# Seven half-tile products in the second and third part of the first two feed forwards, their modulation moved into the first part, and a gate activation scaled by GpSimd

## What is computed

```
def swiglu(h, w_gu, w_down):
    g, u = jnp.split(h @ w_gu, 2, axis=-1)
    return (jax.nn.silu(g) * u) @ w_down
...
        h = h + swiglu(rms_norm(h, f_norm[layer]), f_w_gu[layer], f_w_down[layer])
```

## Time and profile before

| | us |
|---|---|
| median of 3 runs | 2104.94 (2104.70 to 2105.11) |
| the profiled execution | 2104.22 |
| its span, first to last instruction | 2102.3 |
| TensorE busy | 2074.3 (99%) |
| TensorE weight loads busy | 1675.8 (80%) |
| VectorE busy | 1137.5 (54%) |
| ScalarE busy | 813.9 (39%) |
| GpSimd busy | 863.0 (41%) |

### The profile page before, as it was taken

The page is one execution under the profiler, slowest core; times in us unless marked ns, Lnnn a source line. Parts: engine busy times, 40 slices in busy tenths (PEclk is TensorE's granted clock), DMA queues, the critical chain, the costliest instruction groups (busy, mean ns, idle before and its releaser), DMA issues.

```text
span 2102.3 us, 27305 instructions
## 1 busy us (share of the span) xinstructions
PE 2074.3 (99%) x10570; PEld 1675.8 (80%) x10570; DVE 1137.5 (54%) x1785; ACT 813.9 (39%) x1243; POOL 863.0 (41%) x644
## 2 busy tenths in 40 slices
PE   8999999999999999999999999999999999999999
PEld 6888888888888444888888878676778888989898
DVE  6445542343354797445325355576664847749393
ACT  4123221222323787322122245564454535435252
POOL 5545655555542211455556534322223240342333
PEclk9999999999999999999999999999999999999999
DMA  4224333432541000243343231211112122233232
GB/s 174 100 100 150 120 140 138 160 114 77 192 131 55 21 1 7 105 159 135 130 155 120 84 123 60 81 41 60 58 43 80 42 83 98 71 111 111 91 108 93
DMA packets 35529, 206.20 MB, mean 98 GB/s; under 512 B 4192, under 2 KB 5344, under 8 KB 16096
## 3 DMA queue, kind: packets, MB, share of 16 engines
q1 hardware_dynamic: 33408, 197.89, 26.2%
q10 hardware_dynamic: 2016, 6.88, 1.0%
HBM read 200.63 MB, written 2.10 MB: 96 GB/s over the span
## 4 chain that ended last, share of the span: by engine, by line
issue 39%; PE 32%; POOL 27%; ACT 1%; DVE 0%; DMA 0%; POOLq 0%; SPq 0%; DVEq 0%; ACTq 0%
POOL WL L523 27%; PE PS L1274 9%; PE PS L895 2%; PE PS L926 2%; PE PS L908 2%; PE PS L1340 2%; PE PS L1341 2%; PE PS L1342 2%; PE PS L634 2%; PE PS L636 2%; PE PS L635 2%; PE PS L718 1%; PE PS L720 1%; PE PS L719 1%; PE PS L825 1%
## 5 line engine op out<-in xcount | busy, mean ns | idle before, releaser
L523 POOL TENSOR_TENSOR WL<-WR,WH 128x512 fp32r<-128x512 f32 (+2 forms) x528 | 703.9, 1363 | 887.2 <-ACT WH L1409 887.2
L634 PE MATMUL PS<-Hh,WH 128*128 128x512 f32 x1152 | 451.8, 392 | 9.2 <-DVE Hl L2052 7.9
L1409 ACT ACTIVATE WH<-WR 128x2048 fp32r<-128x2048 f32 (+2 forms) x133 | 237.6, 1786 | 561.5 <-PE PS L636 521.1
L635 PE MATMUL PS<-Hl,WH 128*128 128x512 f32 x1152 | 449.4, 390 | 0.0
L636 PE MATMUL PS<-Hh,WL 128*128 128x512 f32 x1152 | 449.3, 390 | 0.0
L634 PEld LDWEIGHTS PS<-Hh,WH 128*128 128x128 f32 x1152 | 216.9, 188 | 56.3 <-issue 9.0
L635 PEld LDWEIGHTS PS<-Hl,WH 128*128 128x128 f32 x1152 | 217.0, 188 | 45.8 <-issue 1.0
L636 PEld LDWEIGHTS PS<-Hh,WL 128*128 128x128 f32 x1152 | 217.0, 188 | 45.5
L634 PE MATMUL PS<-Gh,WH 128*128 128x512 f32 x416 | 161.8, 389 | 0.0
L635 PE MATMUL PS<-Gl,WH 128*128 128x512 f32 x416 | 161.8, 389 | 0.0
L636 PE MATMUL PS<-Gh,WL 128*128 128x512 f32 x416 | 161.8, 389 | 0.0
(11 more groups left out here) (354 smaller groups left out, 3717.7 us busy)
## 6 DMA issues: line engine op xcount, KB each, us to landing
WR<-wA SPq DMA_DIRECT2D x125, 1024.0 KB, 4.8
AW<-wada SPq DMA_DIRECT2D x24, 1024.0 KB, 6.9
...
```

The costliest lines, as they stand in the source:

```text
L523: ins = nc.gpsimd.tensor_tensor(WL[:, s, piece], WR[:, s, piece], WH[:, s, piece].bitcast(F32), ALU.subtract)
L634: nc.tensor.matmul(PS[:, b, :], wh[:, c, cols], pe_h, start=c == 0, stop=False)
L635: nc.tensor.matmul(PS[:, b, :], wh[:, c, cols], pe_l, start=False, stop=False)
L1409: nc.scalar.activation(WH[:, s, 0:n], WR[:, s, 0:n], ACT.Copy).then_inc(hi_s, 1)
```

## The change

- The feed forwards of layers 0 and 1 are made in three parts, of 8, 8 and 6 hidden tiles, as that of layer 2 is. The first part stays plain; all of the second and third part (14 units of each layer) are made of seven products.
- In these units `gate_sums` gets a second instruction, the multiplication with the row of inverse roots (now `RSF`), which waits for the first. The multiplication after the silu is given to GpSimd (`scale_gate`), and `gated` waits for it.
- GpSimd's order in a part: from the third unit on, the scaling for unit n-2 comes ahead of the two weight sums of unit n; the scalings of the last two units come after the last sums, ahead of the low parts of the down weights.
- All 12 modulation units of a layer are done in its first part: one behind each of the 8 gate and up units, four among the first part's down products. The two sums of one share an output buffer, so the second waits for the first. SyncE issues their loads accordingly.
- In the first part GpSimd also adds high and low input together (`whole_inputs`, eight 128x512 additions behind the third and fourth unit), VectorE makes the four sums of token halves (behind the fourth unit) and their low parts (behind the sixth and seventh), ScalarE the high parts.
- The down weights of the first part use other buffers (`DNH`, `DNL` for odd units). The weights of the second part's first unit can be put in place after seven of the eight down tiles.
- In layer 2 the instructions stay; the host lays the weights out in quarters for the new units.

```
 SEGMENTS = [
     ("win", "A", 12), ("wout", "A", 4),
-    ("gu0a", "A", F1), ("dn0a", "B", 8), ("gu0b", "A", F2), ("dn0b", "C", 8),
+    ("gu0a", "A", 8), ("dn0a", "D", 8), ("gu0b", "A", 8), ("dn0b", "D", 8), ("gu0c", "A", 6), ("dn0c", "E", 8),
     ("wq", "A", 4), ("wkv", "A", 6), ("wo", "A", 4),
-    ("gu1a", "A", F1), ("dn1a", "B", 8), ("gu1b", "A", F2), ("dn1b", "C", 8),
+    ("gu1a", "A", 8), ("dn1a", "D", 8), ("gu1b", "A", 8), ("dn1b", "D", 8), ("gu1c", "A", 6), ("dn1c", "E", 8),
...
-SEVEN = [(SEGS["gu2" + half], k) for half, n in LAST for k in range(PLAIN if half == "a" else 0, n)]
+PARTS = [("a", 8), ("b", 8), ("c", 6)]
+SEVEN = [(SEGS[f"gu{l}{part}"], k) for l in range(3) for part, n in PARTS for k in range(n)
...
                 if name in ("gu0a", "gu1a"):
-                    segment_with_ada(name, 12 * int(name[2]), (1, 3, 5, 7, 9, 11))
+                    segment_with_ada(name, 12 * int(name[2]), {0: 1, 1: 1, 2: 3, 3: 4, 4: 5, 5: 6, 6: 7})
                 elif name in ("dn0a", "dn1a"):
-                    segment_with_ada(name, 12 * int(name[2]) + 6, (3, 6))
-                elif name in ("gu0b", "gu1b"):
-                    segment_with_ada(name, 12 * int(name[2]) + 8, (1, 3, 5, 7))
+                    segment_with_ada(name, 12 * int(name[2]), {7: 0, 8: 1, 9: 2, 10: 4, 11: 5})
                 else:
                     segment(name)
...
-                if n >= 2:
+                if nth(n) >= 2 or layer(n) < 2:
                     pool.wait_ge(tile_s, TILES_AFTER[u - 2])
                 nc.gpsimd.tensor_tensor(sums[:, W_S2, :], sums[:, W_S1, :], raw[:, A11, :], ALU.add).then_inc(s2_s, 1)
+
+            def scale_gate(n):
+
+                pool.wait_ge(sg_s, hidden(n) + 1)
+                nc.gpsimd.tensor_tensor(SG[:, n % 2, :], SG[:, n % 2, :], RSF[:, :], ALU.mult).then_inc(scaled_s, 1)
 
...
+            def whole_inputs(l, m0):
+
+                h, low = HHL[l]
+                pool.wait_ge(h_s, DC * (1, 4)[l] + DC)
+                for m in range(m0, m0 + 4):
+                    nc.gpsimd.tensor_tensor(HN[l][:, m, :], h[:, m, :].bitcast(F32), low[:, m, :].bitcast(F32),
+                                            ALU.add).then_inc(sh_s, 1)
+
+            def first_part(l):
+
+                seg = SEGS[f"gu{l}a"]
+                for u in range(seg.units):
+                    s, n = u % 2, seg.size // 4
+                    pool.wait_ge(hi_s, seg.unit0 + u + 1)
+                    for j in range(4):
+                        piece = slice(j * n, j * n + n)
+                        ins = nc.gpsimd.tensor_tensor(WL[:, s, piece], WR[:, s, piece], WH[:, s, piece].bitcast(F32),
+                                                      ALU.subtract)
+                    ins.then_inc(lo_s, 1)
+                    if u in (2, 3):
+                        whole_inputs(l, 4 * (u - 2))
...
             for name, _, _ in SEGMENTS:
-                if name in ("gu2a", "gu2b", "gu2c"):
-                    for n, (seg, _) in enumerate(SEVEN):
-                        if seg.name == name:
-                            sum_two(n)
-                            sum_four(n)
-                elif name in ("dn2a", "dn2b", "dn2c"):
-                    last_down(name[3])
+                if name in ("gu0a", "gu1a"):
+                    first_part(int(name[2]))
+                elif name[0:2] == "gu":
+                    of_part = units_of(int(name[2]), name[3])
+                    for n in of_part:
+                        if int(name[2]) < 2 and n > of_part[1]:
+                            scale_gate(n - 2)
+                        sum_two(n)
+                        sum_four(n)
+                    if int(name[2]) < 2:
+                        scale_gate(n - 1)
+                        scale_gate(n)
+                elif name[0:2] == "dn":
+                    down_low(int(name[2]), name[3])
                 else:
                     segment(name)
...
+                    for c in range(seg.chunks):
+                        if n is not None and m == 0 and c == 2:
+                            product4(n)
+                        if m == 0:
+                            g_ready(c)
...
+                act.wait_ge(tile_s, seven_tiles(n - 2) if nth(n) >= 2 else first_free(n))
+                if l < 2 and nth(n) == 0:
+                    act.wait_ge(tile_s, SEGS[f"dn{l}a"].tile0 + DC - 1)
+                if l < 2 and nth(n) == 1:
+                    act.wait_ge(ada_acc_s, 12 * l + 12)
...
+                sums_high(FIRST[l], W_S3, s13_s, h13_s)
+                sums_high(FIRST[l], W_S2, s4_s, h24_s)
+                quarters_high(FIRST[l])
...
+                if nth(n) < 2:
+                    dve.wait_ge(evac_s, seven_tiles(n) - 2)
+                ins = nc.vector.tensor_tensor(SG[:, n % 2, :], SNA[:, n % 2, :], PS[:, 5 + 2 * (n % 2), :], ALU.add)
+                if layer(n) < 2:
+                    chain.mark(ins)
+                    chain.wait()
+                    ins = nc.vector.tensor_tensor(SG[:, n % 2, :], SG[:, n % 2, :], RSF[:, :], ALU.mult)
+                ins.then_inc(c1_s, 1)
...
+                dve.wait_ge(sg_s, hidden(n) + 1)
+                if layer(n) < 2:
+                    dve.wait_ge(scaled_s, n + 1)
+                dve.wait_ge(tile_s, seven_tiles(n))
...
+            def down_part(l, part, first, ada=()):
+
+                seg = SEGS[f"dn{l}{part}"]
+                late = l < 2 and part == "a"
+                for m in range(DC):
+                    if late and m == DC - 1:
+                        quarters_low(first)
+                        sums_low(first, W_S2, h24_s, lo_s)
...
+                    if m in ada:
+                        a = 8 + ada.index(m)
+                        modulation_unit(12 * l + a, a)
+                    if first is not None and m == 5:
+                        sums_one_three(first)
+                    if late and m == 6:
+                        sums_low(first, W_S3, h13_s, l13_s)
...
+            def first_part(l):
+
+                seg = SEGS[f"gu{l}a"]
...
+                    modulation_unit(12 * l + u, u)
+                    if u == 3:
+                        combine_tokens(l, (T1, T3, T2, T4))
+                    if u in (5, 6):
+                        for i in ((T1, T2), (T3, T4))[u - 5]:
+                            combined_low(l, i)
...
+                root_known()
+                first_part(l)
+                down_part(l, "a", FIRST[l], (1, 2, 4, 5))
+                seven_part(l, "b")
+                down_part(l, "b", units_of(l, "c")[0])
+                seven_part(l, "c")
...
                 for b in range(2):
+                    if b:
+                        chain.wait()
                     ins = nc.vector.tensor_tensor_reduce(
-                        out=AWC[:, b, :], in0=AW[:, slot, b * D:b * D + D], in1=CROW[:, :], scale=1.0, scalar=0.0,
+                        out=AWC[:, :], in0=AW[:, slot, b * D:b * D + D], in1=CROW[:, :], scale=1.0, scalar=0.0,
```

784 lines of the change are left out of this document (396 added, 388 removed).

## The result

| | before | changed |
|---|---|---|
| median of the runs shown with it, us | 2105.03 (2104.70 to 2105.89, 4 runs) | 2164.91 (2164.08 to 2165.68, 4 runs) |
| ratio to before, 95% interval | | 1.0284 (1.0266 to 1.0302) |
| span of the profiled execution, us | 2102.3 | 2163.9 |
| mean granted clock of TensorE | | 0.990 |

The changed kernel is 59.9 us slower, where +34.5 was forecast. The direction is right, and the time lies above the range of 2118 to 2150.

What follows compares the result with a forecast made beforehand. TensorE, busy 99% of the span, was taken as the bound. Terms -22.7 + 30.4 + 19.6 + 3.0 + 4.2 = +34.5 us on 2104.2 gave 2138.7 us, range 2118 to 2150.

Steps and rivals of the forecast that it cites:

- 14 units of seven products: TensorE, layers 0 and 1: a seven-product unit takes 10.07 us against 10.88 plain; 22.7 us less over 28 units.
- first part: GpSimd's low parts, additions and modulation holds need 32.6 us where 30.5 pass: 2.1 late, 4.2 us for both layers.
- seam first to second part: First seven-product weights, behind the seventh down tile, come about 1.5 us late; 3.0 us in two layers, bounds 0 and 5 each.
- second part, its opening included: Part of 8 units: 8.4 us lost to VectorE's slower loop, plus 0.8 for VectorE starting behind.
- third part: Part of 6 units: last unit's wait ends at 56.3 us against 50.3 for TensorE alone, 6.0 lost.
- two seams to down products: First down weights' low part waits behind GpSimd's last scaling: TensorE waits 4.9 us, four seams, 19.6 us more.
- The loop: VectorE in seven-product units: `gated` 4.12 us after the gate sums plus 7.20 gives 11.32 us per unit.
- the rival without hold-up: GpSimd's scaling not held up by VectorE: loop 10.75 us, 13.6 us less in all, 2125 us; chance 0.23.
- The clock: Rival: TensorE's clock falls after idling 4.9 us at each of four seams, 2.7 us each, 2149 us; chance 0.18.
- The ends of the layers: Down products are the same number of matmuls in three parts as in two; no cost was forecast.
- waits on `U`: Sign: TensorE waits for `U` some 24 times, 1.0 to 1.3 us each in the middle of a part.
- L600: Sign: this line of GpSimd's gate scaling takes a mean near 1.9 us, not 1.3.

Runs made afterwards that it cites:

- number 7: Changed kernel with inputs normalised ahead: `HN` holds `X` times gain times `RSF`, no `RSF` multiplication left in the loop; 2108.63 us, ratio 1.0017.
- Numbers 5: Changed kernel with the `RSF` multiplication of the gate sums before the silu left out in layers 0 and 1, second and third parts; 2143.93 us, ratio 1.0188.
- Number 1: Changed kernel with GpSimd making the first down weights' low part before the last unit's gate scaling, not after; 2140.97 us, ratio 1.0167.
- number 2: Changed kernel with 18 and 16 small matmuls of ones keeping TensorE busy before the later parts' down products, layers 0 and 1; 2155.19 us, ratio 1.0233.
- Number 6: Changed kernel with layers 0 and 1 cut into parts of 8, 6 and 8 units instead of 8, 8 and 6; 2160.82 us, ratio 1.0266.
- number 9: Changed kernel with layer ends changed: VectorE makes `wq`'s first low part; `qkv`'s second moves behind `ACCF`, its first in four pieces; 2158.10 us, ratio 1.0249.
- number 3: Changed kernel with the whole inputs `HN` of layers 0 and 1 made by ScalarE instead of GpSimd; 2162.75 us, ratio 1.0267.
- number 12: Changed kernel with `HN` by ScalarE and VectorE's combining sums spread over units 5 and 6, following copies and differences likewise; 2164.30 us, ratio 1.0278.

## Why the prediction was wrong

The sum for one layer, by its terms, against layer 0 of the changed kernel (us):

| term | predicted | measured |
|---|---|---|
| 14 units of seven products | -11.35 | -11.35 (the pace without waits, number 7) |
| first part | 2.1 | 4.9 |
| seam first to second part | 1.5 | 2.7 |
| second part, its opening included | 9.2 | 9.1 |
| third part | 6.0 | 5.4 |
| two seams to down products | 9.8 | 4.7 + 4.1 |
| slow clock behind the two seams | none | 2.6 + 2.7 |
| end of the layer | none | 4.3, and 2.2 by the slow clock behind it |
| **sum** | **17.2** | **31.4** |

From its start to the second tile of `wq` the changed layer 0 is in fact 31.0 us longer. Layer 1 is 30.4 longer, to the first product of `qkv`; its end costs 7.6.

- **The loop: right.** 11.32 was forecast and is 11.13, of it 4.11 for 4.12 up to `gated`. The scaling was held up by VectorE's sum, as the earlier trace rows said; the rival without hold-up would have shown a pace of 10.75. Numbers 5 and 7 took the two multiplications away one after the other: 21.0 us and, with the seams, 56.3.
- **The seams: right** within 0.8 us (4.7 and 4.1 for 4.9; the second part has the larger low parts). Number 1 removed these waits by order alone.
- **The clock: the step that failed first.** I wrote it down as a rival with 2.7 us a seam and 0.18 of chance, because no row showed a gap of 4.9. It happened at all four, and number 2 priced it at 9.7 us; the table has it as 2.6 and 2.7 in layer 0, and it was 1.6 twice in layer 1. The Trainium skill (page "TensorE: Matmul & The Clock Gate", section "HAM oscillation — how this bites in real kernels") says that such gaps bring the clock down; four gaps of 4 to 4.5 us agree, but not the shorter ones of the last section, behind some of which the clock fell as well. With it the forecast would have been 2149. I gave a wait its length and not what the wait does to the matmuls after it.
- **The ends of the layers: missing.** "The down products are the same number of matmuls in three parts as in two" is true, and I priced it at nothing without naming what the long last part had covered. Its tiles went from 6.8 us to 4.08, and the two chains behind them, the load of `wq`'s first unit and VectorE's queue at the end of layer 1, came late by 4.3 (and 2.2 of slow clock) and 7.6. This is some 14 us, the largest part of the miss of 25. Number 6, which made the last tiles longer, and number 9, which made the chains shorter, each cut both waits.
- **The first part: mis-sized** by 2.8 a layer (4.9 for 2.1). The queue on GpSimd, from the third unit's low part to the fifth's, took 199.40 to 232.83, 33.4 us for the 32.6 of the sum, and the waits on it and beside it (0.85 and 1.85) cost 3.0 from start to start. The rest is a wait that no term had: I left out the four combining sums on VectorE. They occupy it for 8.1 us (number 3), hold GpSimd's low part beside them, and stand in front of the sums that the silu waits for, behind which ScalarE's high part waits. In the changed kernel this shows as the wait of 0.89; with the additions gone it was 1.75 (number 3), and spreading the sums took it away (number 12). Some 0.8 us is in no single wait.
- **The seam from first to second part**: 2.7 for 1.5, inside the bounds of 0 and 5, but not by the forecast's reason. Only 0.7 of it stands in front of the first weights of seven products (recorded wait 0.54). Another 1.5 are two waits among the first part's down products, on the last gate (0.62) and on `DNL` (0.58), which were in no term. No run was made for it.

Of the signs named, these came: 22 waits on `U` (for 24), four on L641 (4.5 and 4.0, not 4.9), L600 at 1.88 inside a part, L2363 idle in front of it, and 0.43 behind the seams. The waits on `U` are 0.8 in the records where I said 1.0 to 1.3: the loop is 0.2 shorter, and a record counts idle time only from the modelled end of the matmul before.
